# Other nominal times and other fetch runs for a planned decoder-layer kernel

## The reference

```python
z = einsum('ntd,dc->ntc', x, w_in)            # 1024 -> 5192 columns
u = a * sigmoid(b)                            # 512 channels, causal depthwise conv of 31 taps
conv = silu(layer_norm(conv1d(u))) @ w_conv_out
idx = top_k(indexer_scores(qi, wi, ki), 128)  # 256 for the samples
attn = sparse_attend(q, k[idx], v[idx])       # 16 heads, 4 kv heads
m = sigmoid(g_conv) * conv + sigmoid(g_attn) * attn
h = layer_norm(ALPHA * x + m @ w_out)
# PEER: 8 heads x 16 experts of 16384 for each token
q1, q2 = split(h @ w_query); s1 = q1 @ keys1; s2 = q2 @ keys2
eidx, g = top 16 of the sums of the two top 16s, softmax
a = gelu(einsum('nd,nhed->nhe', h, peer_u[eidx]))
f = einsum('nhe,nhed->nd', g * a, peer_v[eidx])
y = layer_norm(ALPHA * h + f)
```

## Time and profile before

| | us |
|---|---|
| timed runs, median of 3 | 2060.43 (2060.42 to 2067.68) |
| profiled execution, its own time | 2049.36 |
| its span, from first to last instruction | 2047.4 |
| PE busy | 1264.5 |
| DVE busy | 1288.3 |
| POOL busy | 1172.7 |
| ACT busy | 338.0 |
| mean granted TensorE clock | 0.763 of full speed |

### The profile page before, as it was taken

The page is one execution under the profiler, slowest core; times in us unless marked ns, Lnnn a source line. Parts: engine busy times, 40 slices in busy tenths (PEclk is TensorE's granted clock), DMA queues, the critical chain, the costliest instruction groups (busy, mean ns, idle before and its releaser), DMA issues.

```text
span 2047.4 us, 19306 instructions
## 1 busy us (share of the span) xinstructions
PE 1264.5 (62%) x6055; PEld 556.7 (27%) x6055; DVE 1288.3 (63%) x3102; ACT 338.0 (17%) x900; POOL 1172.7 (57%) x1143
## 2 busy tenths in 40 slices
PE   8997998886741766665367596752322244765425
PEld 4563443452410224332021252410100011221101
DVE  5329979971266867947668499375498996013341
ACT  1510020221100541200044221100100001100000
POOL 1005446735565566656666566566476677446675
PEclk9998998988875885687688657876566556888768
DMA  8819989978999899999999999999799959999997
GB/s 335 339 60 392 338 312 366 333 251 308 339 363 358 329 351 360 402 345 357 356 406 379 337 350 394 339 374 370 243 387 342 403 213 396 361 364 381 372 364 298
DMA packets 213504, 699.49 MB, mean 342 GB/s; under 512 B 27573, under 2 KB 55733, under 8 KB 206579
## 3 DMA queue, kind: packets, MB, share of 16 engines
q0 software_dynamic: 162560, 598.44, 77.7%
q1 hardware_dynamic: 43691, 90.66, 12.3%
q10 hardware_dynamic: 7152, 9.17, 1.2%
HBM read 685.66 MB, written 12.94 MB: 341 GB/s over the span
## 4 chain that ended last, share of the span: by engine, by line
DVE 32%; PE 25%; issue 18%; DMA 7%; POOL 6%; another core or an unknown queue 5%; ACT 3%; SPq 3%; DVEq 0%; ACTq 0%; POOLq 0%
DVE rings L2464 14%; PE acc L2008 6%; POOL rings L1010 6%; DMA rings<-peer_v,late 3%; PE bank L1698 3%; PE bank L1724 3%; PE bank L1573 2%; DVE small L2074 2%; DVE uah L2077 2%; PE acc L1490 2%; DVE zt L2274 2%; DMA conv_acc<-causal 1%; DVE conv_acc L2274 1%; DMA w_conv_out_s<-cache_kT 1%
## 5 line engine op out<-in xcount | busy, mean ns | idle before, releaser
L1010 POOL DMA_INDIRECT rings<-peer_u,late x544 | 608.6, 1119 | 417.6 <-DVE late L2464 154.1
L1010 POOL DMA_INDIRECT rings<-peer_v,late x544 | 530.9, 976 | 327.3 <-issue 137.3
L2008 PE MATMUL acc<-rings,z_stages 128*32 128x512 f32 x2048 | 364.9, 767 | 390.5 <-DMA rings<-peer_v,late 162.3
L2464 DVE CUSTOM_DVE_ANT_0 rings<-rings,wide 128x1024 f32<-128x1024 f32 x256 | 299.7, 1216 | 27.6 <-DMA rings<-peer_u,late 15.6
L2008 PEld LDWEIGHTS acc<-rings,z_stages 128*32 128x32 f32 x2048 | 86.1, 130 | 640.3 <-issue 637.3
L2464 DVE CUSTOM_DVE_ANT_0 rings<-rings,uah 128x1024 f32<-128x1024 f32 x160 | 191.6, 1222 | 86.8 <-DMA rings<-peer_u,late 72.8
L2464 DVE CUSTOM_DVE_ANT_0 rings<-rings,late 128x1024 f32<-128x1024 f32 x128 | 153.7, 1221 | 8.4 <-DMA rings<-peer_u,late 6.9
L1523 PE MATMUL acc<-rings 128*128 128x512 f32 (+1 forms) x352 | 155.6, 591 | 4.2 <-DMA rings<-w_in 3.4
L1424 ACT COPY z_stages<-late 128x4 f32<-128x4 f32 x136 | 25.4, 197 | 433.6 <-remote 232.9
L1854 PE MATMUL bank<-keep,soft_score 128*128 128x64 f32 x288 | 63.5, 389 | 49.6 <-ACT soft_score L1235 27.9
L1523 PEld LDWEIGHTS acc<-rings 128*128 128x128 f32 x352 | 66.4, 203 | 77.6 <-issue 73.3
(11 more groups left out here) (316 smaller groups left out, 1705.1 us busy)
## 6 DMA issues: line engine op xcount, KB each, us to landing
rings<-w_in SPq DMA_DIRECT2D x35, 1024.0 KB, 8.7
rings<-w_out POOLq DMA_DIRECT2D x32, 512.0 KB
rings<-peer_u,late POOLq DMA_INDIRECT x544
rings<-peer_v,late POOLq DMA_INDIRECT x544
z_rows<-z_stages ACTq DMA_DIRECT2D x30, 256.0 KB
soft_score<-ln SPq DMA_DIRECT2D x6, 1024.0 KB
zt<-z_rows SPq DMA_DIRECT2D x2, 2596.0 KB
rings<-w_out POOLq DMA_DIRECT2D x4, 1024.0 KB, 7.6
```

What stands on the lines that cost most here:

```text
L1010: nc.gpsimd.indirect_dma_start(ring[:, place, :], None, table, offs).then_inc(row_in[place], 16)
L2008: last = nc.tensor.matmul(acc_v[QUAD * j:QUAD * (j + 1), half * BLK:(half + 1) * BLK], lone[:, quad % LONE, j, QUAD - 1 - m:2 * QUAD - 1 - m],
L2464: V.tensor_tensor_reduce(out=ring[:, place, :], in0=ring[:, place, :], in1=h, scale=1.0, scalar=0.0, op0=ALU.mult, op1=ALU.add, accum_out= ...
```

## The change

All nominal times are given anew, and the u and v runs of the three mixed stages are others. No piece of work is added or taken away; `merge`, `homes` and the waits are as they were. The stages start 6.519 us later on the nominal scale, and are as long. The whole diff:

```diff
--- before.py
+++ after.py
@@ -407,12 +407,10 @@
     LAST = N_TILES - 1
     Q_SLOTS = SLOTS // 4
 
-    MIXED_FROM, STAGE, SLOT_US, LANDING, LANDING_MIXED = 515.0, 350.0, 1.37, 9.0, 13.0
-    EARLY_V = (64, 48, 48, 48)
-    OUT_LEAD, EARLY_USE = 30.0, 8
-    BLOCKS = {1: ((0, 12), (10, 16), (17, 4), (20, 32), (81, 0)),
-              2: ((0, 16), (10, 20), (17, 8), (20, 36), (81, 0)),
-              3: ((0, 16), (10, 24), (32, 4), (42, 36), (44, 0))}
+    MIXED_FROM, STAGE, SLOT_US, LANDING, LANDING_MIXED = 521.519, 350.0, 1.317, 4.532, 14.458
+    EARLY_V = (68, 52, 52, 48)
+    OUT_LEAD, EARLY_USE = 28.207, 8
+    BLOCKS = {1: ((4, 24), (4, 4), (23, 0), (24, 16), (73, 16)), 2: ((0, 32), (16, 0), (13, 24), (30, 12), (69, 8)), 3: ((16, 28), (6, 16), (26, 0), (4, 32), (76, 0))}
 
     def step_at(t):
 
@@ -421,9 +419,9 @@
     def fetches():
 
         for k in range(SLOTS):
-            yield 160.0 + 2.2 * min(k, 44) + 1.85 * max(k - 44, 0), ("u", 0, k)
+            yield 165.481 + 2.206 * min(k, 44) + 1.912 * max(k - 44, 0), ("u", 0, k)
         for i in range(EARLY_V[0]):
-            yield 426.0 + 1.37 * i, ("v", 0, i)
+            yield 424.027 + 1.224 * i, ("v", 0, i)
         for t in range(1, N_TILES):
             order, k, i = [], 0, EARLY_V[t - 1]
             for n_u, n_v in BLOCKS[t]:
@@ -459,23 +457,11 @@
                 lag -= SLOT_US * (number - N_QUADS + 1)
             yield at + lag, table, tile, number
 
-    CLOCK_0 = ((0.0, 29.0), (0.02, 31.0), (0.03, 33.0), (0.28, 62.0), (0.33, 68.0), (0.34, 70.0), (0.47, 86.0),
-               (0.482, 88.0), (0.497, 93.0), (0.51, 96.0), (0.537, 104.0), (0.541, 104.5), (0.549, 107.0),
-               (0.558, 108.0), (0.56, 109.0), (0.618, 122.5), (0.62, 123.0), (0.63, 124.5), (0.635, 126.6), (0.638, 127.2),
-               (0.645, 129.0), (0.65, 129.0), (0.67, 136.0), (0.69, 145.0), (0.70, 150.0), (0.705, 151.0), (0.71, 156.0),
-               (1.0, 276.0))
-    CLOCK_1 = ((0.0, 256.0), (0.012, 268.0), (0.015, 269.0), (0.02, 270.0), (0.028, 272.0), (0.045, 278.0), (0.05, 280.0),
-               (0.09, 292.0), (0.14, 312.0), (0.165, 321.0), (0.2, 334.0), (0.48, 412.0), (0.497, 416.0), (0.51, 419.0),
-               (0.537, 428.0), (0.541, 429.0), (0.549, 432.0), (0.558, 436.0), (0.56, 437.0), (0.618, 453.0), (0.63, 458.0),
-               (0.638, 461.0), (0.648, 464.0), (0.65, 465.0), (0.69, 490.0), (0.70, 495.0), (0.71, 499.0), (0.982, 583.0),
-               (1.0, 587.0))
-    CLOCK_T = ((0.0, 0.0), (0.012, 8.0), (0.02, 10.0), (0.05, 21.0), (0.09, 34.0), (0.2, 100.0), (0.48, 175.0),
-               (0.497, 180.0), (0.51, 183.0), (0.537, 192.0), (0.541, 193.0), (0.549, 196.0), (0.558, 200.0),
-               (0.56, 201.0), (0.618, 219.0), (0.63, 224.0), (0.638, 227.0), (0.648, 230.0), (0.65, 231.0),
-               (0.69, 249.0), (0.70, 253.0), (0.71, 256.0), (0.982, 343.0), (1.0, 347.0))
-    CLOCK_S = ((0.0, 0.0), (0.04, 32.0), (0.21, 56.0), (0.48, 176.0), (0.84, 272.0), (0.845, 282.0), (1.18, 323.0),
-               (1.3, 338.0))
-    FRONT_LAG, FINISH_LAG, LN2_LAG = 72.0, 301.0, 20.0
+    CLOCK_0 = ((0.0, 29.0), (0.02, 31.0), (0.03, 32.62), (0.28, 61.55), (0.33, 72.0), (0.34, 72.01), (0.47, 88.05), (0.482, 90.05), (0.497, 95.05), (0.51, 107.4), (0.537, 110.95), (0.541, 116.13), (0.549, 118.93), (0.558, 118.94), (0.56, 118.95), (0.618, 118.96), (0.62, 118.97), (0.63, 118.98), (0.635, 118.99), (0.638, 119.0), (0.645, 119.01), (0.65, 119.02), (0.67, 119.03), (0.69, 122.65), (0.7, 134.75), (0.705, 142.8), (0.71, 147.16), (1.0, 272.43))
+    CLOCK_1 = ((0.0, 256.0), (0.012, 268.0), (0.015, 272.63), (0.02, 272.75), (0.028, 276.03), (0.045, 281.43), (0.05, 283.43), (0.09, 283.44), (0.14, 314.84), (0.165, 321.66), (0.2, 334.66), (0.48, 412.66), (0.497, 424.05), (0.51, 424.06), (0.537, 427.56), (0.541, 440.28), (0.549, 440.29), (0.558, 445.44), (0.56, 448.17), (0.618, 464.72), (0.63, 469.42), (0.638, 469.43), (0.648, 470.44), (0.65, 470.45), (0.69, 488.23), (0.7, 499.48), (0.71, 504.0), (0.982, 584.87), (1.0, 589.58))
+    CLOCK_T = ((0.0, 0.0), (0.012, 6.69), (0.02, 6.7), (0.05, 22.89), (0.09, 22.9), (0.2, 89.35), (0.48, 167.1), (0.497, 171.3), (0.51, 175.65), (0.537, 180.59), (0.541, 186.24), (0.549, 193.24), (0.558, 197.06), (0.56, 197.07), (0.618, 214.38), (0.63, 215.16), (0.638, 218.31), (0.648, 222.72), (0.65, 226.71), (0.69, 244.71), (0.7, 247.75), (0.71, 251.33), (0.982, 338.33), (1.0, 355.79))
+    CLOCK_S = ((0.0, 0.0), (0.04, 21.24), (0.21, 45.99), (0.48, 169.77), (0.84, 267.92), (0.845, 276.97), (1.18, 321.12), (1.3, 321.13))
+    FRONT_LAG, FINISH_LAG, LN2_LAG = 71.371, 298.978, 19.725
 
     def nominal(t, x):
 
@@ -498,7 +484,7 @@
 
     def second_at(k):
 
-        return 122.6 + 14.0 * k if k < 0.25 else 146.0 + 11.6 * (min(k, 10.0) - 0.25) + 15.4 * max(k - 10.0, 0.0)
+        return 122.6 + 14.0 * k if k < 0.25 else 148.825 + 11.661 * (min(k, 10.0) - 0.25) + 13.86 * max(k - 10.0, 0.0)
 
     N_TARGETS = N_TILES
     SECOND = (4, 5, 6, 0, 1, 2, 3, *range(7, N_BLK + 1))
```

## The result

The changed kernel is slower: 2084.56 us median of 4 runs (2076.52 to 2089.77) against 2060.43 (2049.67 to 2067.68, 4 runs), a ratio of 1.0104 with a 95% interval of 1.0069 to 1.0140. Two more measurements gave 1.0090 [1.0058, 1.0123] and 1.0101 [1.0042, 1.0159]. The forecast was 2044.4 us with a range of 2010 to 2080.

A forecast was written before the change was run, and what follows sets the result against it. No engine's busy share bounds it; DMA is nearly full from 150 us, with time lost in its holes. Terms -6 - 8 - 5 + 3 = -16 us took 2049.36 to 2033.4; plus 11.07 gave 2044.4 us, range 2010 to 2080.

The forecast's parts named there:

- part 2: Stages 1 and 2: new runs of u and v rows shorten POOL's waits; -8 us, bounds -18 and +6.
- Part 1: End of the second pass: half 20 runs alone, first peer_v gather sooner, w_out pieces behind it; -6 us, bounds -14 and +3.
- Tile 0's clock: Second pass: four matmul calls move behind tile 0's query product; nothing, bounds -2 to +3.
- Part 3: Start of the sample tile, hole at 1440 to 1460: shorter hole, fewer dots bursting; -5 us, bounds -15 and +8.
- Part 4: Stage 3, samples' top-k: DVE bounds it, dots put off behind a run where it idles; +3 us, bounds 0 and +17.
- The samples' tail: Last fetches: clock some 4 to 10 us earlier, fetch order from 920 on the same; nothing, bounds -5 and +5.
- The rival that came in by sign: Tile 3: dot bursts starve gathers of descriptors, two more long gathers; +18 us to 2078 us, chance 0.22.

The follow-up runs named there:

- e3: Kernel before with one line changed, the new nominal times of the second pass; ratio 0.9943 to the kernel before.
- k2: Changed kernel with index products and scores of tiles 2 and 3 spread over 13 us by one CLOCK_T number; ratio 0.9991 to the kernel before.
- h5: Changed kernel with index products and scores spread for tiles 2 and 3 and for tile 1 too; ratio 1.0008 to the kernel before.
- e1: Changed kernel with all runs (BLOCKS, EARLY_V) of before, index scores still on one point; ratio 1.0117 to the kernel before.
- h2: Changed kernel with index scores of tiles 2 and 3 spread and all runs (BLOCKS, EARLY_V) of before; ratio 1.0008 to the kernel before.
- f2: Kernel before with one CLOCK_T number changed, index products and scores of tiles 2 and 3 on one point; ratio 1.0077 to the kernel before.
- g1: Kernel before with the new second-pass times, new CLOCK_1 and new times of the first v fetches; ratio 0.9969 to the kernel before.
- e5: Changed kernel with the runs of stages 1 and 2 of before, index scores still on one point; ratio 1.0007 to the kernel before.
- f1: Changed kernel with index products and scores of tiles 2 and 3 spread over 13 us by one CLOCK_T number; ratio 0.9951 to the kernel before.
- i5: The same program as f1, measured on the quicker chip; ratio 0.9866 to the kernel before.

## Why the prediction was wrong

- **The step that failed** is in part 2: "The rest of the clocks of tiles 2 and 3 shifts by 5 us less [...] Nothing, bounds -3 to +3." The sum compared when the pieces start, not what stands between them. The collapse of 13 us of nominal time into 0.01 measured +0.4 to +1.1%, that is 8 to 23 us, in pairs that differ in it alone. That is the sign of the result: without it the kernel is at 0.9951 and 0.9991, where the forecast was 0.992.
- **"DVE is half idle in these stretches [...], so more u rows cost it nothing"** failed in part for the same reason. DVE's idle time was real, but it was spent behind a score that waited for ACT and PE, and a u row in the ring behind it can't use it. Price taken: -8; measured: nothing with spread scores, a loss with dense ones. The gain is there in fetches 160 to 512 and is lost again in 544 to 640, by what the prediction had as its bound of +6, "v rows beside attention" that hold places: POOL waits 15.58 and 9.13 us there, and DMA over 1140 to 1180 fell to 0.54. The hole at 690 to 700 did go, as foreseen, and a wider one opened at 640 to 680.
- **Part 1** had the mechanism (half 20 runs alone; w_out behind the same wait, 439.46) and a size far too small in the profile: -6 against -20. The last z copy came 30.6 us earlier (462.27 to 431.70), not 14.0, since the later halves of the second pass lie closer (13.86 instead of 15.4): SP's last load of w_in starts at 403.66 instead of 422.66, 19 us that no term held. The output product started at 463.65, not behind 474, and routing at 550.72 was early. In the whole kernel e3 puts that line at -0.6%, 12 us, with an interval from 0.2 to 0.9%.
- **Tile 0's clock** and the new first u time: +4.2 us at the first gather (bounds +3), and -1.8 by fetch 128. Small, as said.
- **Part 3** was forecast at -5 and came out at +6.2 (fetches 768 to 800). PE's wait did shrink (41.2 to 32.24 us, under 38) and the gather beside the dots too (9.41 to 6.27), but POOL waited 27.09 instead of 23.60: SP came to the sample loads 23 us later (1443.05 to 1466.22), and 15 of these POOL's list had lost before fetch 768. But e3, with the lists of before, needed 85.2 us here, and executions with the new ones 74.0 (k2) to 85.1 (h5): the hole differs between executions by as much as the term.
- **Part 4** had the wrong sign: +3 against -7.4. DVE was busy 140.06 of 150 us and could take more: 147.05 after. e1 and h2, with the old runs and the new clocks, took 167.4 and 166.4 us for fetches 800 to 896, as the new runs did (167.6), and e3, f2 and g1, with the old clocks, 169.7 to 174.6; so the gain seems to be the clocks', which were not tried apart here. "DVE bounds it" was read from a share of 93%.
- **The samples' tail**, "nothing, bounds -5 and +5", lost 11.1. Ten profiled executions with the new clocks took 361.1 to 373.2 us for fetches 896 to 1119; with the old ones before, f2 and e3 took 355.0 to 355.9 and g1 361.2. It wasn't tried by itself: a cause that is only seen.
- **The rival that came in by sign** (slower, 2078) came in for another reason. Its mechanism, one dot burst more, did not: the long gathers are 6.27 and 16.58 us, in the places of the old 9.41 and 17.73. That 2078 lies near the 2084.56 measured is chance. The Trainium skill (SBUF — State Buffer, "SBUF: two separate sides") lets a gather starve beside VectorE's work; the 16.58 us row agrees once more (dots without a gap from 1664.13 to 1681.32 beside it), but longer pure u runs gave no second such row.

## What to carry to other kernels

In a program of in-order queues merged by nominal times, compare not only when each piece moves but what stands between the pieces: list, for each chain that hops between engines (product, relu, score), the independent work laid between its links. A chain laid on one point makes each engine stand for the others, and an idle share there is no room for more rows. The same holds for rows laid behind such a chain on another engine: the new runs moved v rows behind attention on PE, and POOL stood for their places. A gain at one hole is worth what the next stages keep: in the two profiled executions, of 21.8 us at fetch 160 the changed kernel had 15.6 left at fetch 512 and none at 640.

## What the hardware showed

- After a wait of 9.77 us PE ran at 0.50 of its clock for at least the 20 us from 1060 to 1080, though busy all of it; the same kind of block was run at full clock (1.12 us a pair) in the kernel before. From the first filter pair behind the wait to the next v row it took 31.9 us in e1 (1050.85 to 1082.72), and 19.2 in e5 (1044.35 to 1063.56), at full clock.
- The same program (f1, k2, i5) took a median of 1891.70 us on one chip and 2072.73 and 2056.20 on two others, with the same bytes and instructions; DMA was at 1.01 and 1.03 instead of 0.92 and 0.89 in the two stretches shown.
- On those four chips the kernel before spread over 2035 to 2115 us from run to run, so single profiles differ by more than most terms of the sum; only the ratios tell them apart, and those from about 0.8% on.
